# Fast matrix product in a decoder's feed-forward stages: two weight sums of each block by an accumulating DMA, activation sums and residual adds on VectorE, the third chunk's down projection plain

## The reference

```python
def swiglu(h, wg, wu, wd):
    return (jax.nn.silu(h @ wg) * (h @ wu)) @ wd
for i in range(DEPTH):
    x = x + 0.5 * swiglu(rmsnorm(x, norm_ffn1[i]), w_ffn1_gate[i], w_ffn1_up[i], w_ffn1_down[i])
    x = x + mixer_i(rmsnorm(x, norm_mix[i]))      # layer 0: latent attention, layer 1: gated short convolution
    x = x + 0.5 * swiglu(rmsnorm(x, norm_ffn2[i]), w_ffn2_gate[i], w_ffn2_up[i], w_ffn2_down[i])
```

## Time and profile before

| | us |
|---|---|
| median of 3 runs (2544.06 to 2547.26) | 2545.67 |
| the profiled execution's own time | 2545.28 |
| its span | 2543.5 |
| TensorE matmul busy | 2337.7 |
| VectorE busy | 1947.0 |
| GpSimd busy | 1101.3 |

### The profile page before, as it was taken

The page is one execution under the profiler, slowest core; times in us unless marked ns, Lnnn a source line. Parts: engine busy times, 40 slices in busy tenths (PEclk is TensorE's granted clock), DMA queues, the critical chain, the costliest instruction groups (busy, mean ns, idle before and its releaser), DMA issues.

```text
span 2543.5 us, 47588 instructions
## 1 busy us (share of the span) xinstructions
PE 2337.7 (92%) x17745; PEld 2234.6 (88%) x17745; DVE 1947.0 (77%) x2594; ACT 1235.5 (49%) x2234; POOL 1101.3 (43%) x660
## 2 busy tenths in 40 slices
PE   6899998999999999998899988899997999799997
PEld 6898988976899999998898987899987999799997
DVE  7989898556555555547989899989898656898987
ACT  4545555364455555534545454545454223455554
POOL 3586865000000000004586856586865000677674
PEclk8999999989999999989999999999999999999999
DMA  3233323310211111212333322233332333233332
GB/s 110 83 98 95 99 83 109 88 49 27 59 32 48 48 43 43 59 30 73 89 95 94 99 81 82 77 99 96 96 89 79 92 92 92 60 99 92 100 90 78
DMA packets 372781, 200.21 MB, mean 79 GB/s; under 512 B 31168, under 2 KB 369174, under 8 KB 372552
## 3 DMA queue, kind: packets, MB, share of 16 engines
q1 hardware_dynamic: 372372, 197.03, 26.8%
q10 hardware_dynamic: 180, 0.11, 0.0%
HBM read 194.27 MB, written 2.87 MB: 78 GB/s over the span
## 4 chain that ended last, share of the span: by engine, by line
PE 44%; POOL 19%; DVE 15%; issue 13%; ACT 7%; DMA 0%; DVEq 0%; SPq 0%; POOLq 0%; ACTq 0%
PE ps L2023 15%; PE ps L932 4%; POOL xT L827 4%; PE ps L532 4%; DVE pairs L788 4%; PE ps L536 4%; PE ps L534 4%; POOL wsum L710 3%; POOL wsum L705 3%; PE ps L934 3%; PE ps L933 3%; POOL wsum L709 3%; POOL wsum L707 3%; ACT pairs L782 2%; DVE mixes L728 1%
## 5 line engine op out<-in xcount | busy, mean ns | idle before, releaser
L932 PE MATMUL ps<-hs,w_hi 128*128 128x260 f32 x1512 | 434.7, 287 | 59.5 <-ACT mixes L1012 41.2
L933 PE MATMUL ps<-hs,w_hi 128*128 128x260 f32 x1512 | 427.3, 283 | 0.0
L934 PE MATMUL ps<-hs,w_lo 128*128 128x260 f32 x1512 | 427.2, 283 | 0.0
L932 PEld LDWEIGHTS ps<-hs,w_hi 128*128 128x128 f32 x1512 | 284.3, 188 | 75.7 <-issue 61.8
L705 POOL TENSOR_TENSOR wsum<-raw 128x512 f32<-128x512 f32 (+1 forms) x124 | 176.6, 1424 | 374.9 <-DVE w_lo L681 283.1
L933 PEld LDWEIGHTS ps<-hs,w_hi 128*128 128x128 f32 x1512 | 285.4, 189 | 0.0
L934 PEld LDWEIGHTS ps<-hs,w_lo 128*128 128x128 f32 x1512 | 284.8, 188 | 0.0
L710 POOL TENSOR_TENSOR wsum<-raw,wsum 128x512 f32<-128x512 f32 (+1 forms) x124 | 269.7, 2175 | 0.0
L2070 ACT ACTIVATE ksq<-ps 128x384 f32<-128x384 f32 (+1 forms) x384 | 146.8, 455 | 197.2 <-PE ps L2023 197.2
L932 PE MATMUL ps<-hs,x_hi 128*128 128x260 f32 x728 | 208.7, 287 | 29.4 <-ACT mixes L1012 11.7
L709 POOL TENSOR_TENSOR wsum<-wsum,raw 128x512 f32<-128x512 f32 (+1 forms) x124 | 225.7, 1820 | 9.7
(11 more groups left out here) (394 smaller groups left out, 7006.1 us busy)
## 6 DMA issues: line engine op xcount, KB each, us to landing
raw<-in_w_ffn_gate SPq DMA_DIRECT2D x88, 512.0 KB, 3.8
raw<-in_w_ffn_up SPq DMA_DIRECT2D x88, 512.0 KB, 3.8
raw<-in_w_ffn_down SPq DMA_DIRECT2D x64, 512.0 KB, 4.0
cache<-in_cache_latent SPq DMA_DIRECT2D x128, 128.0 KB, 2.0
raw<-in_w_ffn_down SPq DMA_DIRECT2D x32, 384.0 KB, 3.3
raw<-in_w_conv_in SPq DMA_DIRECT2D x24, 512.0 KB, 3.9
raw<-in_w_o_attn SPq DMA_DIRECT2D x8, 512.0 KB, 4.1
cache<-in_cache_krope SPq DMA_DIRECT2D x128, 32.0 KB, 1.8
```

The lines of the kernel that those rows point to most:

```text
L932: nc.tensor.matmul(o, hi[:, kc], mh[:, xc], start=start and k == 0, stop=False, skip_group_check=goes_on)
L933: nc.tensor.matmul(o, hi[:, kc], ml[:, xc], start=False, stop=False, skip_group_check=goes_on)
L934: mm = nc.tensor.matmul(o, lo[:, kc], mh[:, xc], start=False, stop=last, skip_group_check=goes_on)
```

## The change

1. **Weight sums.** For each S and D block SyncE issues a DMA within SBUF (`sums_begin`) that copies the first halves of both raw rows (g1, u1) into `wsum75` or a second buffer `wsum75b`; it waits first for both loads. GpSimd waits for the copy and issues a DMA that adds the up row (u1, u2) onto it, which gives g1+u1 and u1+u2. GpSimd then makes only s6 and s3. Signs change to fit.
2. **Mixes.** The sums of the four sets at a stage's start are made by VectorE, and the last two of the three operations become `scalar_tensor_tensor`. `keep_third` writes into `acc`, and no longer waits for the pairs.
3. **x additions.** GpSimd's additions to `xT` are made by VectorE.
4. **Third chunk.** Its S blocks make no mixes; its down projection is 8 plain tiles of 6 pieces by 6 matmuls (`down_tile`), 288 matmuls instead of 252, without weight sums, each followed by its part of the next norm.
5. **Order at the start.** VectorE's order up to block 3 is written anew, and the first pair's mixes and split move into block 3.

```diff
         def weight_sums(pool, bk):
-            u1, u2, g1, g2 = bk.raw_half(1, 0), bk.raw_half(1, 1), bk.raw_half(0, 0), bk.raw_half(0, 1)
-            for j in (1, 0):
-                bk.loaded(pool, j)
+            g1, g2 = bk.raw_half(0, 0), bk.raw_half(0, 1)
+            pool.wait_ge(sums_in, 16 * (bk.s + 1))
+            pool.dma_start(bk.sums()[:], bk.raw_row(1), accum_op=ALU.add).then_inc(sums_added, 16)
             if ahead:
-                pool.wait_ge(part_lo_made, ahead.end(M75, 2))
-            nc.gpsimd.tensor_tensor(s5, u1, u2, ALU.add).then_inc(sums_made, 1)
-            pool.wait_ge(sums_made, 4 * bk.s + 1)
+                pool.wait_ge(part_lo_made, ahead.end(M63, 2))
+            pool.wait_ge(sums_added, 16 * (bk.s + 1))
             nc.gpsimd.tensor_tensor(s6, s5, g1, ALU.add).then_inc(sums_made, 1)
-            pool.wait_ge(sums_made, 4 * bk.s + 2)
+            pool.wait_ge(sums_made, 2 * bk.s + 1)
             nc.gpsimd.tensor_tensor(s3, s6, g2, ALU.add).then_inc(sums_made, 1)
-            nc.gpsimd.tensor_tensor(s7, u2, s6, ALU.subtract).then_inc(sums_made, 1)
...
+        def sums_begin(sp, bk):
+            for j in range(2):
+                bk.loaded(sp, j)
+            if bk.b == 4:
+                sp.wait_ge(set_made, own_sets(bk.at, KH))
+                sp.wait_ge(part_used, blocks[bk.at][2].done)
+            elif bk.b > 4:
+                sp.wait_ge(part_lo_made, blocks[bk.at][bk.b - 2].end(M75, 2))
+            r = bk.raw_slot(0)
+            sp.dma_start(bk.sums()[:].rearrange("p (h c) -> p h c", h=2), raw[:, r:r + 2, 0:bk.width]).then_inc(sums_in, 16)
...
+            def first_out(bk):
+                x = xT[:, 2 * bk.d * T:(2 * bk.d + 1) * T]
...
+                nc.vector.tensor_tensor(x, x, gate_t[:], ALU.add).then_inc(first_added, 1)
...
+            def down_tile(bk):
...
+                for k in range(LAST):
+                    if bk.j == 0:
+                        pe.wait_ge(set_made, pair_sets(at, PAIRS_ALL * at + 8) + k + 1)
+                    kc = slice(k * P, (k + 1) * P)
+                    mm = product(bk.j % 4, hi[:, kc], lo[:, kc], last2_hi, last2_lo, k, k == 0, k == LAST - 1)
+                mm.then_inc(part_used, bk.size)
...
             def keep_third(bk):
                 act.wait_ge(part_used, bk.end(M75))
-                if not bk.out:
-                    act.wait_ge(set_made, pair_sets(at, bk.pair))
...
-                nc.scalar.copy(bk.first(), ps[:, bk.bank, 0:HALF]).then_inc(kept, 1)
+                nc.scalar.copy(bk.third(), ps[:, bk.bank, 0:HALF]).then_inc(kept, 1)
```

More of the change, by code:

```diff
@@ L458, in first, with third, sums @@
             def first(self):
-                x = OA if self.out or self.odd else EA
+                x = OA if self.odd else EA
                 return mixes[:, x * HALF:(x + 1) * HALF]
+            def third(self):
+                return acc[:, self.b % 2 * HALF:(self.b % 2 + 1) * HALF]
+            def sums(self):
+                return (wsum75b, wsum75)[self.b % 2]
             def second(self):
@@ L486, in build @@
             if s[:3] == "ffn":
-                owners += [("block", bk, y) for bk in blocks[FFN_AT[int(s[-1])]][1:] for y in range(2)]
+                owners += [("block", bk, y) for bk in blocks[FFN_AT[int(s[-1])]][1:] for y in range(bk.loads)]
         def raw_free(sp, r):
@@ L725, in first_mix @@
[L725 to L739 removed]
+            ins.then_inc(mixed, 1)
@@ L791, in ffn_sp, with kept_tile @@
+        def kept_tile(bk):
+            own = blocks[bk.at]
+            old = own[bk.b - 1]
+            if bk.b == 3:
+                return own[1]
+            if old.kind == "S":
+                return old if (old.pos if old.last else old.odd) else None
+            if bk.kind == "S" and bk.last:
+                return next(z for z in own if z.kind == "S" and z.last)
+            return None
         def ffn_sp(sp, i, u0):
@@ L953, in block @@
-                half_product(bk, M12, A, EB, not late, True, rest).then_inc(part_used, 1)
-                half_product(bk, M12 + 1, B, OB, not late, True, rest).then_inc(part_used, 1)
+                if bk.out and bk.d == 0:
+                    pe.wait_ge(set_made, pair_sets(at, PAIRS_ALL * at + 4 * (bk.c + 1)))
+                half_product(bk, M12, A, EB, True).then_inc(part_used, 1)
+                half_product(bk, M12 + 1, B, OB, True).then_inc(part_used, 1)
                 pe.wait_ge(part_lo_made, bk.end(M63, 2))
@@ L1026, in block @@
+            def block(bk):
+                nxt, done = own[bk.b + 1], kept_tile(bk)
                 m75_hi(act, bk)
-                if bk.last_pair:
-                    pair_hi(act, old, MIX_PART)
                 keep_first(bk)
                 m4_hi(act, bk)
-                if old.kind == "S" and old.odd and not bk.last_pair:
-                    pair_hi(act, old)
-                if shown:
-                    publish_hi(act, n + 1, k)
+                if done:
+                    last_hi(act, done) if done.last else pair_hi(act, done)
@@ L1162, in after @@
             def after(bk):
                 if bk.out:
-                    tile_out(bk)
+                    second_out(bk)
                 else:
-                    hid(bk) if bk.kind == "S" else plain_hid(bk)
+                    hid(bk)
             def block(bk):
-                old, nxt = own[bk.b - 1], own[bk.b + 1] if bk.b + 1 < BLOCKS else None
-                shown = more and bk.out and bk.c == 2 and bk.d > 0
-                k = 2 * bk.d - 2 if bk.out else 0
-                pair = old.kind == "S" and old.odd
@@ L1173, in block @@
-                after(old)
-                if pair:
-                    pair_mix(dve, old)
-                if bk.last_pair:
-                    pair_lo(dve, old, RAW_PART)
-                    pair_lo(dve, old, MIX_PART)
+                old, nxt, done = own[bk.b - 1], own[bk.b + 1], kept_tile(bk)
+                early = bk.b > 3
+                if early:
+                    after(old)
+                    if done and not done.last:
+                        pair_mix(dve, done)
                 m75_lo(dve, bk)
```

463 lines of the change are left out of this document (213 added, 250 removed).

## The result

The changed kernel takes 2513.59 us (median of 4 runs, 2504.84 to 2519.46) against 2544.86 us before; the ratio is 0.9876, 95% interval 0.9855 to 0.9898. It is 31 us (1.2%) faster; the forecast was 57 us faster. The profiled execution took 2519.46 us, 25.8 us less than the profiled one of before.

The account below looks back on a forecast made before the run. The new two-block chain of DMAs was taken as the bound. Three stages at 5.0 + 0.35 + 1.0 + 9.5 and one at 5.0 + 0.35 + 1.0 + 3.0 save 56.9 us: 2545.28 becomes 2488, range 2390 to 2585.

Parts of the forecast that it names:

- The chain over two blocks: Up weights' load, copy, accumulation, sums, rounding and split bound the loop: 22.9 us per two blocks with mixes, 21.4 without.
- slope of 48 us per us of chain: Each us more or less in the two-block chain is worth 12 x 4 = 48 us until another bound takes over.
- not fast: Fast-DMA rival: copy 2.9 us, accumulation about 3, loops at TensorE's 19.9 us; total 2379 to 2400 us; chance 0.27.
- 6 x 22.94 + 6 x 21.39 = 266.0: Block 4 to 28 of a stage: six two-block steps with mixes, six without; 266.35 us before, gain 0.35 a stage.
- slow rival: Loads, copy and accumulation share the DMA engines; copy 3.8 and accumulation 7.6 us give 2598 us; chance 0.23.
- they need not collide: Argument against slow DMAs: the trace has the DMA engines far from full, so transfers need not collide.
- between blocks 28 and 29: One more block goes from 11.34 to about 10.3 us because its own chain is ahead: gain 1.0 a stage.
- the third chunk: Block 29 to stage end: 36 more matmuls but TensorE's waits removed; gain 9.5 us in three stages, 3.0 in ffn3.
- The start: Stage start to block 4: fourth set split at 1204 not 1209.6, block 4's L1117 at 1222.0 not 1227.07; gain 5.0.
- split hidden: Pair's split moved into block 3 is hidden under block 4's chain; with a fast DMA it costs up to 2.05 + 1.55.
- VectorE as the bound: Rival: two remaining GpSimd operations block VectorE as much as four did, S blocks stay at 11.33 us: 2472 us; chance 0.07.

Follow-up runs that it names:

- plain-DMA run: Changed kernel with its accumulating DMA made a plain copy of the same 512 KB, additions s7 and s5 left out (output not the product): 2450.84 us, ratio 0.9646.
- kernel with VectorE's sums: Changed kernel without DMAs within SBUF: VectorE makes s7 and s5 in one addition of 1024 columns, GpSimd keeps s6 and s3: 2489.47 us, ratio 0.9795.
- last kernel that replaces the DMAs: VectorE makes s7 and s5, with that addition right behind `m75_lo` and the pair's split behind `m63_lo` of the next block, against the changed kernel: 2480.12 us, ratio 0.9749.
- kernel with GpSimd's four sums: Changed kernel with part 1 undone: GpSimd makes all four weight sums from the raw rows, no DMA within SBUF: 2533.37 us, ratio 0.9962.
- half-DMA kernel: Changed kernel with only s7 made by a copy and an accumulating DMA of 256 KB each, GpSimd making s5, s6 and s3: 2504.38 us, ratio 0.9856.

## Why the prediction was half right

**The sign and the bound were right.** The chain over two blocks took the place of VectorE and GpSimd as the limit, as the plain-DMA run and the tight links show. In steps with mixes its terms stood at 4.14 us for the load (forecast 3.9), 3.62 for the copy (3.4), 5.17 for the accumulation (5.7), 3.30 for the sums (3.1) and 6.89 for the rest with the rounding (6.84): 23.12 against 22.94. The slope of 48 us per us of chain was 63 / 1.5 = 42 in the plain-DMA run. The accumulation was not fast: 4.8 to 5.0 us, against 3.4 without the addition. The fit cited in the prediction (the Trainium skill, DMA: Bandwidth & Descriptors, "Anatomy of one DMA — SWDGE (gpsimd) path"), 3.2 us for 512 KB, is near what a plain copy on GpSimd's queue took, 3.4; the adding one took 4.9. The Trainium skill (Collectives: The Full Stack, "The bandwidth ceiling") has a reducing step, which reads two sources, at half the rate of a copying one, and the queue's time here, 12.9% against 6.2%, agrees.

**The step that failed is the sum 6 x 22.94 + 6 x 21.39 = 266.0.** Steps without mixes did not take 21.4 us: in even D blocks they took 22.2, in odd blocks 22.7 to 23.1, so all 100 steps, those with mixes included, had a mean of 22.83. The load took 4.7 to 5.0 us there, not 3.9, in S blocks as in D blocks, and the odd blocks' sums 3.6 to 4.0 us, not 3.1, as many fall beside the pair's split and mixes. The load was late where it met the other block's accumulation: in steps with mixes it was in flight beside one for 0.8 us and landed in 4.1, in odd S blocks for 2.7 us and landed in 4.8. Before, all three kinds of row landed in 3.8 to 4.0. I had followed one chain and forgotten the other: blocks b and b + 1 each have one, on the same DMA engines (71% busy in the loop, 33% before), the same GpSimd and the same two queues. The sentence in my slow rival, "they need not collide", was the error. It made the loops 5.7 us a stage longer than worked out, 23 us in all. The profiled execution is 31 us behind the forecast: these 23, 15.5 at the start of the stages and 2 between blocks 28 and 29, less 6.7 that the third chunk gave beyond the forecast and 2.5 in mla. These last two are in part luck, for nothing in the forecast had worked them out.

**The start (5.0 a stage, measured 0.3 to 1.9).** In ffn1 the fourth set was ready 37.5 us after the norm, 2.1 later than worked out: its terms were those of a VectorE left alone, and L748 and L756 took 2.46 and 1.67 us beside block 3's sums on GpSimd, where the same lines took 1.42 and 0.70 just after. From there the copy and the accumulation took 9.8 us instead of 9.1, and the two sums 4.75 instead of 3.1, since the pair's split that moved into block 3 runs beside them. I had called that split hidden. The kernel with VectorE's sums did not do better there (59.7 to 63.8 us from norm to block 4), but TensorE waited 5.28 us in its block 3 of ffn1 for a keep behind the pair's rounding, so what the shared buffer costs isn't shown. The two lines, beside GpSimd's sums and alone:

```profile
1183.28 2.46 DVE L748 SCALAR_TENSOR_TENSOR scaled<-xT,gain,inv 128x520 f32<-128x520 f32 x2
1185.77 1.67 DVE L756 TENSOR_TENSOR scaled<-scaled 128x520 f32<-128x520 f32 x1
...
1183.43 1.75 POOL L732 TENSOR_TENSOR wsum<-wsum,raw 128x512 f32<-128x512 f32 x1 [7.87 <-DVE w_lo L663]
...
1190.24 1.42 DVE L748 SCALAR_TENSOR_TENSOR scaled<-xT,gain,inv 128x520 f32<-128x520 f32 x2
1191.70 0.70 DVE L756 TENSOR_TENSOR scaled<-scaled 128x520 f32<-128x520 f32 x1
```

**The third chunk** gained 10.4 us in ffn1 where 9.5 was worked out, 2.7 in ffn3 where 3.0 was, and 14.7 in ffn2, where I had used ffn1's number: luck, for I had not looked at ffn2, whose stretch took 62.0 us before and not 56.9. TensorE unbroken, as said.

**The rivals.** VectorE as the bound was wrong for this change (192 of 277 us busy), but it is nearly all of the step in the last kernel that replaces the DMAs. The slow rival named the right mechanism, transfers that share the DMA engines, at too high a price.

## What to carry to other kernels

Relieving an engine pays only as far as what replaces it has slack in latency, not only in bandwidth: here two DMAs of 3.5 and 5 us, one behind the other, made a chain of 22.8 us for two blocks that TensorE alone could do in 19.9, while one VectorE operation of 1.22 us for the same sums was 24 us better. When a loop is double-buffered, follow both chains, and ask which of one's transfers fall beside the other's. And where two engines block each other, look at what the added operations meet, not only at how many they are.

## What had not been expected of the hardware

A pause of TensorE can cost more than itself. In the kernel with GpSimd's four sums, before and after the wait of 3.19 us, and then further on:

```profile
1375.00:1378.60 3.60, 3.60 (x31) 3.39 (x29) 3.50 (x5) 0.62 (x1) 3.52 (x3) 1.00 0.00 0
1381.80:1386.00 4.20, 4.20 (x24) 4.20 (x25) 3.28 (x3) 1.17 (x2) 0.51 (x1) 0.66 0.42 125
1386.00:1390.00 4.00, 4.00 (x36) 4.00 (x35) 3.29 (x6) 2.90 (x4) 2.02 (x2) 1.00 0.46 135
```

The granted clock was 0.66 in the mean just after, part of it at the lower level (1.2 GHz), and 24 matmuls took 4.2 us, 0.175 each against 0.116: 1.4 us on top of the 3.2. Not every pause did that: after one of 3.16 us at 1406.6 the granted clock stayed at 1.00. Mean granted clock of that kernel was 0.965 and of the half-DMA kernel 0.963, against 0.980 of the changed one.

An accumulating DMA of 512 KB within SBUF landed in 4.8 to 5.0 us against 3.4 for a plain one, and kept GpSimd's queue for 0.87 to 1.05 us at its issue, a plain one for 0.57 to 0.74. The changed kernel scatters: block 4 to 28 took 267.8 to 276.5 us in the four stages of one execution, where the kernel with VectorE's sums had 263.1 to 263.4. These DMAs aren't the only thing that does it, for the executions of the kernel with GpSimd's four sums, which has none, ran from 2522 to 2545 us.
